# Moving the odd windows' exponents behind the sigmoids in the second block's recurrence stage

## The reference, cut to what matters

```
u = causal_depthwise_conv_2(u, conv_w, conv_b)
r = sigmoid(block_diag_linear(u, w_a, b_a));  i = sigmoid(block_diag_linear(u, w_x, b_x))
log_a = -8 * r * softplus(-lam);  a = exp(log_a);  b = sqrt(-expm1(2 * log_a)) * (i * u)
h = scan of h[t] = a[t] * h[t-1] + b[t];   y_rnn = h * silu(g_rnn)

m = max(max(scores), sink);   p = exp(scores - m)
denom = sum(p) + exp(sink - m);   out = (p / denom) @ v;   y_attn = out * silu(g_attn)

merged = sigmoid(m_rnn) * (y_rnn @ w_rnn_out) + sigmoid(m_attn) * (y_attn @ w_attn_out)
x = x + merged @ w_o;   return rms_norm_2(x, final_norm_g)
```

## Time and profile before

| | |
|---|---|
| median of 3 runs | 1281.52 us (1281.34 to 1283.18) |
| the profiled execution's own time | 1281.51 us |
| its span, first to last instruction | 1279.8 us |
| TensorE busy | 1265.8 us, 99% of the span |
| VectorE busy | 872.5 us, 68% |
| ScalarE busy | 584.7 us, 46% |
| GpSimd busy | 87.3 us, 7% |
| granted TensorE clock | 0.999 of full speed |

### The profile page before, as it was taken

One profiled execution on the slowest core, in us unless ns is written; L12 is line 12 of the kernel. 1 busy time (PEld: TensorE's weight loads), 2 busy tenths in 40 slices (PEclk: granted clock), 3 DMA queues, 4 the chain that ended last, 5 costly groups with the idle time before them and its releaser, 6 DMA issues.

```text
span 1279.8 us, 15383 instructions
## 1 busy us (share of the span) xinstructions
PE 1265.8 (99%) x5767; PEld 1018.3 (80%) x5767; DVE 872.5 (68%) x1162; ACT 584.7 (46%) x859; POOL 87.3 (7%) x68
## 2 busy tenths in 40 slices
PE   9999999999999999999999999999999999999998
PEld 7888777888888888888888888888877767777886
DVE  6489899899868766666665334675379998654544
ACT  6235466232364443333343223513378888644223
POOL 0000222000000200000000001200012220000000
PEclk9999999999999999999999999999999999999999
DMA  8556222432322333333222222359724455755421
GB/s 284 155 132 171 66 66 67 164 99 85 113 83 83 99 99 99 98 98 98 98 98 99 98 98 67 100 137 220 218 75 125 136 140 141 203 138 148 164 66 66
DMA packets 220906, 153.36 MB, mean 120 GB/s; under 512 B 119688, under 2 KB 196400, under 8 KB 220592
## 3 DMA queue, kind: packets, MB, share of 16 engines
q1 hardware_dynamic: 220832, 152.58, 40.5%
q10 hardware_dynamic: 16, 0.00, 0.0%
HBM read 134.21 MB, written 18.35 MB: 119 GB/s over the span
## 4 chain that ended last, share of the span: by engine, by line
PE 88%; DVE 5%; ACT 3%; issue 2%; DMA 0%; SPq 0%; ACTq 0%
PE PS L1883 87%; ACT WH L708 1%; PE PS L1950 1%; DVE WL L1148 1%; DVE TB L1730 1%; DVE SMALL L1711 1%; ACT S2A L987 0%; DMA STAGE<-in_w_in 0%; ACT S2B L987 0%; DVE YR L1761 0%; DVE SMALL L1716 0%; DVE S2B L1706 0%; ACT UC L1035 0%; ACT L1039 0%; DVE S2A L1706 0%
## 5 line engine op out<-in xcount | busy, mean ns | idle before, releaser
L708 ACT ACTIVATE WH<-STAGE 128x1024 fp32r<-128x1024 f32 x214 | 225.7, 1057 | 532.4 <-PE PS L1883 516.7
L1148 DVE TENSOR_TENSOR WL<-STAGE,WH 128x1024 fp32r<-128x1024 f32 x214 | 277.5, 1299 | 167.6 <-ACT WH L708 167.1
L1883 PE MATMUL PS<-XH,WH 128*128 128x512 f32 x960 | 380.6, 396 | 1.7 <-DVE GS L1802 1.7
L1883 PE MATMUL PS<-XH,WL 128*128 128x512 f32 x960 | 373.9, 389 | 0.0
L1883 PE MATMUL PS<-XL,WH 128*128 128x512 f32 x960 | 373.7, 389 | 0.0
L1883 PEld LDWEIGHTS PS<-XH,WH 128*128 128x128 f32 x960 | 180.2, 188 | 45.0 <-issue 4.9
L1883 PEld LDWEIGHTS PS<-XL,WH 128*128 128x128 f32 x960 | 180.3, 188 | 38.7 <-issue 2.4
L1883 PEld LDWEIGHTS PS<-XH,WL 128*128 128x128 f32 x960 | 180.2, 188 | 38.0
L1883 PE MATMUL PS<-WH,XH 128*128 128x512 f32 x224 | 88.0, 393 | 0.3
L1883 PE MATMUL PS<-WH,XL 128*128 128x512 f32 x224 | 87.2, 389 | 0.0
L1883 PE MATMUL PS<-WL,XH 128*128 128x512 f32 x224 | 87.2, 389 | 0.0
(11 more groups left out here) (290 smaller groups left out, 1783.4 us busy)
## 6 DMA issues: line engine op xcount, KB each, us to landing
STAGE<-in_w_in SPq DMA_DIRECT2D x52, 1024.0 KB, 5.1
STAGE<-in_w_up SPq DMA_DIRECT2D x22, 1024.0 KB, 5.1
STAGE<-in_w_down SPq DMA_DIRECT2D x11, 1024.0 KB, 5.0
probabilities<-TB SPq DMA_DIRECT2D x48, 128.0 KB, 5.8
PT<-probabilities SPq DMA_DIRECT2D x18, 256.0 KB, 5.6
STAGE<-in_w_out SPq DMA_DIRECT2D x4, 1024.0 KB, 5.1
STAGE<-in_w_rnn_out SPq DMA_DIRECT2D x4, 1024.0 KB, 5.3
STAGE<-in_w_attn_out SPq DMA_DIRECT2D x4, 1024.0 KB, 5.3
```

The costliest lines, as they stand in the source:

```text
L708: act.activation(ring(WH, n), staged(n), ACT.Copy).then_inc(hi_done, 1)
L1148: dve.tensor_tensor(ring(WL, n), staged(n), ring(WH, n).bitcast(F32), ALU.subtract)\
L1883: return pe.matmul(out_, lhsT, rhs, start=start, stop=stop, skip_group_check=True)
```

## The change

In ScalarE's loop over j, the exponents of a window stand no longer at every even j up to 30. For j up to 16 they stay only where q = 0 (even windows). Those of the odd windows 1, 3, 5 and 7, which stood at q = 2 (j = 2, 6, 10, 14), are issued at q = 3 (j = 3, 7, 11, 15), after the two sigmoids of the recurrence and the two of the gate. From j = 18 on the order is as it was. No instruction with arithmetic is added or removed, and TensorE, VectorE, GpSimd and the DMA queue keep their lists.

```diff
@@ -1087,7 +1087,7 @@
                     rec_exp(2 * m - 1)
                 if j in (18, 20, 22):
                     rnn_hi({18: (0, 1, 2), 20: (3, 4, 5), 22: (6, 7)}[j])
-                if j % 2 == 0 and j < 32:
+                if j % 2 == 0 and j < 32 and (q == 0 or j > 16):
                     window_exp(j // 2)
                 if q == 0 and 0 < m <= KD // 2:
                     rec_a_square(2 * m - 2)
@@ -1103,6 +1103,7 @@
                             act.wait_ge(yg_ready, m)
                         act.activation(SIG[:, c % 2, :], GT[:, c % 4, :], ACT.Sigmoid)\
                            .then_inc(yg_sig, 1)
+                    window_exp(j // 2)
                 if h >= 0 and h % 16 in (1, 3, 5, 7):
                     merge_gates(h)
                 if j in (36, 37, 38):
```

## The result

The changed kernel takes 1288.58 us (median of 5 runs, 1288.50 to 1289.93), the one before 1281.52. The ratio is 1.0055, with a 95% interval from 1.0043 to 1.0066, so it is slower by about 7.1 us. The forecast was 1287.9 us. The profiled execution took 1288.63 us, with a span of 1286.9 us.

A forecast was written before the change was run, and what follows sets the result against it. The prediction took a closed loop of ScalarE and VectorE up to unit 21 to set the end. 1.9 us in group 0 plus 3 x 1.5 gave 6.4 us on the median 1281.52: 1287.9 us, range 1284.5 to 1290.3.

The forecast's parts named there:

- The bound: From 954.80 to 1080.62 us a closed loop of ScalarE and VectorE sets the pace; TensorE, 99% busy, follows.
- The 1.9 us of group 0: Two added table loads on ScalarE start the second sigmoids at 951.15, not 949.27; the even window's exponents move 1.9 us.
- The 1.5 us of groups 1 to 3: VectorE's inversion waits for the odd window's exponents; the scan's product starts 1.5 us later in each of three groups.
- rival A: Faster: TensorE's early release gains 3.3 us and the loop has slack for the wait; 1278.2 us, chance 0.05.
- What could have given it back: Nothing returns the 1.5 us: ScalarE stays ready 0.6 us before VectorE's maximum, and the 2.33 us stall behind GpSimd doesn't shrink.
- rival D: A table switch costs twice its row; five added loads put 6.4 us on top, 1294.3 us, chance 0.02.
- The wait for `II`: TensorE's waits for the recurrence's second sigmoid, 3.3 us in three pieces, go.
- Waits of some 2 us: New TensorE waits for the convolution ahead of blocks 4 and 6, some 2 us each.
- B: Nothing measurable: the delay counts at TensorE only up to unit 17, 2.4 us, then the loop catches up; 1283.9 us, chance 0.08.
- C: Slower by more: a maximum's small operations meet GpSimd's gate product once more, 2.4 us; 1290.3 us, chance 0.05.

The follow-up runs named there:

- The edit on `rec_square`: Kernel before, with VectorE's two rec_square operations moved right behind the unit's drain at q = 1 of groups 1 to 4: 1276.28 us.
- window 3 alone: Kernel before, with only odd window 3's exponents (unit 7, group 1) moved behind the sigmoids: 1283.18 us.
- the kernel without the loads: Changed kernel with Identity and Copy in place of Exp for windows 1, 3, 5 and 7, so no table load stands around them: 1283.92 us.
- the run with the late inversion: Changed kernel with VectorE's inversion for odd windows 1, 3, 5, 7 behind the next unit's drain (3, 5, 7 also behind the scan): 1287.99 us.
- the run with window 1 alone: Kernel before, with only odd window 1's exponents (unit 3, group 0) moved behind the sigmoids: 1283.50 us.
- the run with window 5: Kernel before, with only odd window 5's exponents (unit 11, group 2) moved behind the sigmoids: 1283.53 us.
- the changed kernel with the edit on `rec_square`: Changed kernel, with VectorE's two rec_square operations moved right behind the unit's drain at q = 1 of groups 1 to 4: 1282.39 us.

## Why the prediction was right

**The bound.** That the chain leaves TensorE between 954.80 and 1080.62, and that the pace is set there by ScalarE and VectorE, was the step on which all depended. The edit on `rec_square` has shown it: an engine that is busy 99% of the span got 5 us faster by moving two operations of another engine.

**The 1.9 us of group 0.** The second sigmoids were placed at 951.15 and stand at 951.22, and the even window's exponents start 1.88 us later (956.26 and 954.38). Alone this move measures 1.93 us at unit 23.

**The 1.5 us of groups 1 to 3.** Measured are 1.5, 2.1 and 1.6 us (3.42 less the 1.9 of group 0, then 5.52 - 3.42 and 7.11 - 5.52); window 3 alone measures 1.61. The mechanism was right in each: drain, second gate sigmoid, load, exponents, inversion, scan. The term mis-sized is that of group 2. I worked it out for group 1 and took it three times, though the window turned in group 2 has half the keys and VectorE arrives 0.5 us sooner. That is most of the 0.7 us by which 6.4 fell short of 7.1. One sentence on rival A was wrong without touching the sum: that VectorE's only waits are for ScalarE's splits, which come later as well. There are also 1.1 us for the first taps in the list, and the splits come sooner relative to VectorE's own work, so that the 0.36 us of waiting for one went.

**What could have given it back.** ScalarE stays ready ahead of VectorE's maximum, by 0.67 us at 988.87 (0.6 forecast), and GpSimd's stall kept its length. The Trainium skill's drain of 1.38 us per switch (ScalarE: Activation LUTs, What ACT_TABLE_LOAD costs) isn't seen in these traces: after the load at 975.73 the exponents start 1.29 us later, and the sigmoid ahead of the load, 0.63 us long, starts 0.65 us before it. From the second gate sigmoid to the exponents it is 1.94 us with the load (975.08 to 977.02) and 0.54 us in the kernel without it (973.29 to 973.83). So a switch costs 1.40 us, the row of its load and the overlap of 0.1 us that two neighbours have without it, and rival D, with its 1294.3 us, is out.

**TensorE.** The wait for `II` went in all groups, as forecast. Waits of some 2 us were expected ahead of blocks 4 and 6; they are 2.16 and 1.05 us. The second is shorter because TensorE had lost time on its own before it, at a lower clock (below). It made no difference to the end, since the loop set that.

**The rivals.** A (1278.2) needed slack in the loop, and even the kernel without the loads has none. B (1283.9) needed the loop to catch up after unit 16; the delay of the scan's product in group 3 and that of unit 23 are the same 7.11 us. C needed a second stall behind GpSimd. There was none in the changed kernel, but the run with the late inversion shows that such a stall lies close by.

**What the forecast left out.** The 1.6 us between the two values of a kernel aren't in it. That both medians, 1281.52 and 1288.58, are of the lower value is luck; one of the five runs after took 1289.93 us.

## What to carry to other kernels

A high busy share doesn't say that an engine sets the pace: look for the stretch in which the chain leaves it, and there cost a move by what it does to the list that the chain runs through, instruction by instruction, the table loads with it. Work out each round of a repeated pattern from its own rows, since a shape that differs in one of them changes the wait. And when two engines wait for each other in turn, an operation whose inputs are long ready but that stands behind three others is the first thing to move.

## What the runs showed of the hardware

**TensorE's clock can fall behind a short wait.** The table of stretches of the changed kernel gives the busy time of each engine, and after that of GpSimd (POOL) the granted clock:

```profile
980.00:1000.00 20.00, 17.16 (x80) 12.89 (x79) 18.00 (x25) 15.86 (x30) 8.44 (x5) 1.00 0.54 142
1000.00:1020.00 20.00, 20.00 (x82) 14.13 (x81) 17.11 (x25) 18.75 (x35) 6.21 (x4) 0.91 0.49 118
...
1070.00:1080.00 10.00, 7.80 (x28) 6.29 (x29) 9.15 (x15) 9.95 (x22) 1.31 (x1) 0.83 0.48 153
```

The clock of 0.91 stands in the stretch behind the wait of 2.16 us that ended at 999.23, the 0.83 in that of the wait of 2.21 us that ended at 1072.20. Each is a part of the stretch at the lower of the two levels (1.2 instead of 2.4 GHz), worth 1.8 us (0.09 x 20) and 1.7 us (0.17 x 10). In steps of 1 us the clock is still 1.00 from 999 to 1000 and then 0.66, 0.50, 0.50 and 0.63; behind the other wait it is 0.50 at once, from 1072 to 1075, and 0.79 in the next step. In the kernel before, the granted clock is 1.00 in all stretches from 915 to 1110 us, also behind its wait of 1.70 us at 1080.62. The two falls are most of the 4.6 us that TensorE is busy longer with the same matmuls. In the changed kernel they cost nothing: behind each of them TensorE still has to wait for the loop, 1.05 us at 1032.05 and 0.74 us at 1087.73.

**Where it costs.** In the run with window 1 alone, TensorE waits 1.7 us for the drain just ahead of unit 23, and in the profiled execution the clock falls behind that:

```profile
1080.00:1090.00 10.00, 8.27 (x34) 6.40 (x31) 9.86 (x17) 7.84 (x12) 0.74 (x1) 0.83 0.56 155
```

From unit 23 on there is no more slack, and the last piece of the chain takes 194.55 us in place of 192.96. In the run with window 5, the same wait (8.29 of 10 us busy) leaves the clock at 1.00, and the piece takes 192.96 us:

```profile
1080.00:1090.00 10.00, 8.29 (x41) 6.60 (x38) 9.86 (x17) 7.82 (x12) 0.71 (x1) 1.00 0.56 155
```

The two differ by 1.6 us, which is the distance of the two values seen in the medians. The profiled executions of the run with window 3 (194.56 us) and of the changed kernel with the edit on `rec_square` (194.52 us) have the longer piece too, and with 1284.67 and 1282.39 us they are among the longer runs of their kernels. The executions of the runs with window 1 (1285.00 us) and window 5 (1283.39 us) fit as well. Why the clock falls after one of these waits and not after the other stays open.
